# Gate stage of the second layer: key scaling, differences and shifts of the logs moved from VectorE to GpSimd

## What is computed

```python
def hgrn_gates(fx, lb):
    log_f = jnp.logaddexp(jnp.log(lb), jnp.log1p(-lb) + jax.nn.log_sigmoid(fx))
    k = (1.0 - lb) * jax.nn.sigmoid(-fx)
    return log_f, k
```

## Time and profile before

| | us |
|---|---|
| median of 3 runs | 4069.83 (4064.1 to 4074.27) |
| the profiled execution, its time | 4068.36 |
| its span | 4066.5 |
| PE busy | 3695.6 (91%) |
| VectorE (DVE) busy | 2607.3 (64%) |
| ScalarE (ACT) busy | 2022.8 (50%) |
| GpSimd (POOL) busy | 1042.4 (26%) |

### The profile page before, as it was taken

The page is one execution under the profiler, slowest core; times in us unless marked ns, Lnnn a source line. Parts: engine busy times, 40 slices in busy tenths (PEclk is TensorE's granted clock), DMA queues, the critical chain, the costliest instruction groups (busy, mean ns, idle before and its releaser), DMA issues. The chain is left out here.

```text
span 4066.5 us, 57429 instructions
## 1 busy us (share of the span) xinstructions
PE 3695.6 (91%) x21576; PEld 2898.5 (71%) x21576; DVE 2607.3 (64%) x3794; ACT 2022.8 (50%) x3880; POOL 1042.4 (26%) x1106
## 2 busy tenths in 40 slices
PE   6999898888999787888789999999898989999998
PEld 5775677777775676767466666678666768888886
DVE  3766567767765486776555555548966776665655
ACT  4544366655544286655344444456644554444444
POOL 0016103732017003610155555500281010111000
PEclk7989899999989898999899999999999999999999
DMA  5100113345200102351100000122003551111344
GB/s 192 42 16 1 39 52 112 129 154 189 69 21 1 54 21 99 119 182 54 31 5 7 9 6 6 36 81 80 9 5 138 189 154 42 60 44 42 110 155 150
DMA packets 211397, 295.44 MB, mean 73 GB/s; under 512 B 74218, under 2 KB 140010, under 8 KB 211124
## 3 DMA queue, kind: packets, MB, share of 16 engines
q1 hardware_dynamic: 210564, 291.57, 21.6%
q0 software_dynamic: 416, 0.05, 0.0%
q10 hardware_dynamic: 144, 0.15, 0.0%
HBM read 261.12 MB, written 30.51 MB: 72 GB/s over the span
## 5 line engine op out<-in xcount | busy, mean ns | idle before, releaser
L563 DVE TENSOR_TENSOR x_low<-buf_a,x_high 128x640 fp32r<-128x640 f32 (+5 forms) x360 | 359.9, 1000 | 307.3 <-ACT x_high L610 290.2
L610 ACT CAST x_high<-buf_a 128x640 fp32r<-128x640 f32 (+5 forms) x360 | 311.0, 864 | 394.8 <-PE ps L670 322.2
L668 PE MATMUL ps<-x_high,w_high 128*128 128x512 f32 (+1 forms) x1184 | 443.4, 375 | 61.5 <-DVE w_low L567 55.9
L669 PE MATMUL ps<-x_low,w_high 128*128 128x512 f32 (+1 forms) x1184 | 436.9, 369 | 0.0
L670 PE MATMUL ps<-x_high,w_low 128*128 128x512 f32 (+1 forms) x1184 | 436.0, 368 | 0.0
L3321 PE MATMUL ps<-w_high,x_high 128*128 128x512 f32 x896 | 362.4, 404 | 53.9 <-DVE w_low L3170 52.0
L3322 PE MATMUL ps<-w_low,x_high 128*128 128x512 f32 x896 | 356.1, 397 | 0.0
L3323 PE MATMUL ps<-w_high,x_low 128*128 128x512 f32 x896 | 355.7, 397 | 0.0
L3170 DVE TENSOR_TENSOR w_low<-w,w_high 128x1024 fp32r<-128x1024 f32 x170 | 226.4, 1332 | 172.7 <-ACT w_high L3262 172.7
L3905 DVE TENSOR_REDUCE mx<-ps 128x1 fp32r<-128x1280 f32 x128 | 190.7, 1491 | 200.2 <-PE ps L3780 199.7
L668 PEld LDWEIGHTS ps<-x_high,w_high 128*128 128x128 f32 x1184 | 226.6, 191 | 109.7 <-DVE x_low L563 64.6
(11 more groups left out here) (451 smaller groups left out, 8910.9 us busy)
## 6 DMA issues: line engine op xcount, KB each, us to landing
w<-in_w_out SPq DMA_DIRECT2D x26, 2048.0 KB, 8.4
w<-in_w_mod SPq DMA_DIRECT2D x24, 2048.0 KB, 9.1
w<-in_w_down SPq DMA_DIRECT2D x15, 2048.0 KB, 7.9
w<-in_w_in SPq DMA_DIRECT2D x26, 1024.0 KB, 5.2
w<-in_w_up SPq DMA_DIRECT2D x22, 1024.0 KB, 7.6
w<-in_w_in SPq DMA_DIRECT2D x6, 2048.0 KB, 8.8
x<-in_x SPq DMA_DIRECT2D x16, 512.0 KB, 8.9
scratch_h<-x SPq DMA_DIRECT2D x8, 512.0 KB
```

The costliest lines, as they stand in the source:

```text
L563: dve.tensor_tensor(part(xl, i)[:, 0:s["tn"]], x_of(s), part(xh, i)[:, 0:s["tn"]].bitcast(F32), ALU.subtract).then_inc(x_low, 1)
L610: act.copy(part(xh, i)[:, 0:s["tn"]], x_of(s)).then_inc(x_high, 1)
L668: pe.matmul(g["out"], lhs[0][:, :], rhs[0][:, :], start=(s["kk"] == 0), stop=False)
L669: pe.matmul(g["out"], lhs[0][:, :], rhs[1][:, :], start=False, stop=False)
```

## The change

The class `Gates` gets a program for GpSimd, issued in the same stage. In the second layer it takes over the key scalings (L3460), the additions (L3468) and the subtractions (L3469). The difference no longer reads the shifted logs: a new constant, row 3 minus row 4 of g, is put in row 7, and e = fx - row 7 is computed from the unshifted logs; the addition of row 4 to fx comes after it and is waited for only at L3475 (`moved_up`). VectorE waits for the difference (`differed`) before the absolute value. In the first layer GpSimd's program returns at once.

```diff
@@ class Beside
+    def pool(self, pool):
+        pass
@@ project_split
+        if beside:
+            @block.gpsimd
+            def _(pool):
+                beside.pool(pool)
@@ Gates.dve, bounds(i), i == KD
                 link(dve.tensor_tensor(g[:, 4, :], g[:, 7, :], g[:, 2, :], ALU.subtract))
+                link(dve.tensor_tensor(g[:, 7, :], g[:, 3, :], g[:, 4, :], ALU.subtract), self.bounded)
@@ Gates.dve, work(direction, o)
-            if self.LB and o in (2, 3):
-                c = o - 2
-                m = 2 * direction + c
-                dve.wait_ge(self.act_chain, acts + c + 1)
-                link(dve.tensor_scalar(key[:, :, c, :], key[:, :, c, :], g[:, 5, m:m + 1], None, ALU.mult))
             if o in (5, 6):
                 c = o - 5
                 dve.wait_ge(self.act_chain, acts + 5 + c)
-                link(dve.scalar_tensor_tensor(fx[:, c, :], fx[:, c, :], 0.0, e[c][:, :], ALU.min, ALU.subtract))
+                link(dve.scalar_tensor_tensor(fx[:, c, :], fx[:, c, :], 0.0, e[c][:, :], ALU.min, ALU.subtract), self.logs)
             if self.LB and o in (6, 7):
                 c = o - 6
                 m = 2 * direction + c
-                link(dve.tensor_scalar(fx[:, c, :], fx[:, c, :], g[:, 4, m:m + 1], None, ALU.add))
-                link(dve.tensor_scalar(e[c][:, :], fx[:, c, :], g[:, 3, m:m + 1], None, ALU.subtract))
+                dve.wait_ge(self.differed, m + 1)
                 link(dve.scalar_tensor_tensor(e[c][:, :], e[c][:, :], -1.0, e[c][:, :], ALU.mult, ALU.max), self.shifted)
             if self.LB and o in (self.added, self.added + 1):
                 dve.wait_ge(self.act_chain, acts + 9 + c)
+                dve.wait_ge(self.moved_up, m + 1)
                 link(dve.scalar_tensor_tensor(fx[:, c, :], fx[:, c, :], g[:, 3, m:m + 1], e[c][:, :], ALU.max, ALU.add))
@@ Gates
+    def pool(self, pool):
+        if not self.LB:
+            return
+        e, g = self.e, self.g
+        pool.wait_ge(self.bounded, 1)
+        for direction in range(2):
+            fx, key = self.a[direction], self.key[direction]
+            acts = self.n_init + self.n_dir * direction
+            for c in range(2):
+                m = 2 * direction + c
+                pool.wait_ge(self.act_chain, acts + c + 1)
+                pool.tensor_scalar(key[:, :, c, :], key[:, :, c, :], g[:, 5, m:m + 1], None, ALU.mult).then_inc(self.scaled, 1)
+            for c in range(2):
+                m = 2 * direction + c
+                pool.wait_ge(self.logs, m + 1)
+                pool.tensor_scalar(e[c][:, :], fx[:, c, :], g[:, 7, m:m + 1], None, ALU.subtract).then_inc(self.differed, 1)
+                pool.wait_ge(self.differed, m + 1)
+                pool.tensor_scalar(fx[:, c, :], fx[:, c, :], g[:, 4, m:m + 1], None, ALU.add).then_inc(self.moved_up, 1)
```

More of the change, by code:

```diff
@@ L3411, in __init__ @@
         self.g = lay("g", [P, 8, 4])
-        self.lb_in, self.dve_chain, self.bounds, self.magnitude, self.shifted, self.act_chain = self.sems = k.sems(
-            "bounds_in", "gates_dve_chain", "bounds_ready", "magnitude", "shifted", "gates_act_chain")
+        (self.lb_in, self.dve_chain, self.bounds, self.bounded, self.magnitude, self.logs, self.differed, self.shifted, self.moved_up, self.scaled,
+         self.act_chain) = self.sems = k.sems("bounds_in", "gates_dve_chain", "bounds_ready", "shifts_ready", "magnitude", "logs_done",
+                                              "differed", "shifted", "moved_up", "keys_scaled", "gates_act_chain")
         self.n_init, self.n_dir = (3, 10) if self.LB else (0, 6)
```

## The result

The changed kernel took 4091.53 us (median of 4 runs, 4087.6 to 4095.35) against 4066.97 (median of 4, 4059.33 to 4074.27) for the kernel before: ratio 1.0057, 95% interval 1.0041 to 1.0073, that is 17 to 30 us slower. The forecast was 4075.6 with a range up to 4090, and no change as the likeliest outcome. Both are wrong. The profiled execution took 4087.6 us (span 4085.8).

The account below looks back on a forecast made before the run. PE and, from 1494 to 1511, VectorE were taken to pace the stage; 10T - 9.2 with T = 1.5 us added 5.8 to the profiled 4068.36, giving 4074.2, and 1.5 to the median made 4075.6; range 4059 to 4090.

Parts of the forecast that it names:

- what bounds the stage: Second layer's projection stage: PE sets the pace where it has splits, VectorE from 1494 to 1511; at most some 12 us.
- the two engines take turns: Gate steps: while GpSimd runs, a VectorE instruction reading two SBUF tensors stands still, one whole instruction at a time.
- Rival 1: Second layer's gate stage: engines work side by side, so removed VectorE time counts; -8.0 us, 4061.8; chance 0.18.
- rival 2: Same stage: engines side by side and PE's clock stays up; -13.1 us, 4056.7, faster; chance 0.06.
- The sum 2 x (4T - 3.68) + 2T - 1.80: Shifts and differences of both directions plus key scalings of direction 1: 10T - 9.2, +5.8 us at T = 1.5.
- T: Time of one of the twelve GpSimd instructions of 128x1280 f32 in the stage; taken as 1.5 us.
- it is nearest to the cast, and I take T = 1.5 us: GpSimd's unseen one-tensor form priced between a cast (1.25 us) and two-tensor work (2.89), near the cast.
- The upper bound: GpSimd's new instruction takes at most the 2.89 us of an operation with two tensors and 1280 columns.
- rival 3: Shifts, both directions: GpSimd as slow as with two tensors, T = 2.89; +19.7 us, 4089.5, slower; chance 0.26.
- The sum by that rule, +1.5: By the skill's line rate at 1.2 GHz, T would be 1.07 us and the sum below +1.5 us.
- Cost: nothing: Key scalings of direction 0, about 1448 to 1453: 1.2 us more fits into 3.7 us of VectorE idle.
- the term 2 x (T - 0.90): Key scalings of direction 1, where VectorE has no idle: +1.2 us.

Follow-up runs that it names:

- copies: The changed kernel with each of GpSimd's twelve instructions replaced by a copy of the same tile: stage 159.4 us, +1.6 against before; kernel ratio 1.0013.
- beside_only: VectorE's program of the kernel before, plus twelve GpSimd tensor_scalar instructions on a tile nobody reads: stage 188.9 us, +31.1; one run, 4108.4 us.
- two_tensor: The changed kernel with GpSimd's twelve instructions as tensor_tensor with a broadcast column: stage 169.9 us, +12.1 against before; kernel ratio 1.0033.
- bench_prices: The kernel before plus an added first stage timing GpSimd forms alone and beside short VectorE instructions: tensor_scalar alone 3.53 us; unchanged gate stage 158.2 us.

## Why the prediction was wrong

**Right: what bounds the stage, and that the two engines take turns.** The forecast rested on the earlier trace rows, and the turns came as written: copies shows them instruction by instruction, and beside_only shows that they alone make the loss. Rival 1 (side by side) and with it rival 2 are out. The sum 2 x (4T - 3.68) + 2T - 1.80 holds, if T is read as the hold: with 1.08 us it gives +1.6 (measured +1.6, copies), with 2.1 us +11.8 (+12.1, two_tensor), with 2.80 us +18.8 (+18.2, the change). In the last, two small errors of the sum cancel: the second absolute value of direction 0 was held for 1.26 us and not 2.80, since the evictions had covered the rest, and the key scalings of direction 0 cost 1.2 us and not nothing.

**Wrong: "it is nearest to the cast, and I take T = 1.5 us".** This is the step that failed. T is 3.52 us alone, and its hold 2.80. I put an unseen form between two seen ones and picked by the number of tensors it reads. The form is what costs: tensor_scalar by a column takes 2.3 us more than a copy of the same tile, and 1.2 us more than the same product as a tensor_tensor with a broadcast column (2.32). Why tensor_scalar is so dear stays open. That VectorE stands still for the *whole* T was off too, the other way: with T = 3.52 the sum would have been +26.0. The upper bound failed as well: tensor_scalar is dearer than two-tensor work, 3.52 against 2.88 us. So rival 3 had the right mechanism and, since its 2.89 us is by accident close to the hold of 2.80, nearly the right time (+19.7 for +18.2). I gave it 0.26 and ended the range at its value, with nothing left for a longer T, so that the measured 4091.5 lies 1.5 us outside.

The Trainium skill's rule that GpSimd runs one-input work at roughly line rate ("GPSIMD Engine Reference", 4.1 Engine selection) is borne out for the copy (1.25 us for an estimated 1.07) and not for tensor_scalar (3.52). The sum by that rule, +1.5, lies near the +1.6 of copies by accident: the copy takes 1.25 us and holds VectorE for 1.08.

**Wrong in a small term: "Cost: nothing" for the key scalings of direction 0.** With 1.5 us they would have fitted into the idle; with holds of 1.85 and 2.79 they opened a gap of 2.03 us in PE at 1460 and cost about 1.2; 1.7 of their net surplus of 2.84 us did fit into the idle. In direction 1 the term 2 x (T - 0.90) is 5.55 - 1.80 = 3.75 us instead of 1.2.

**Wrong by a detail of the turns.** With the long instruction w_low at 1469.78 was not held, though GpSimd had been issued at 1468.67; the log behind it was. With copies w_low was held. The count of holds stays the same. In bench_prices, too, the short VectorE instruction that starts 0.04 us after GpSimd's tensor_scalar (28.38 against 28.34) keeps its 0.18 us, and the next one is held. Why one short instruction passes is not settled.

The kernel's own difference is 24.6 us between medians (17 to 30 by the interval) for 18.2 in the stage and 1.0 ahead of it in the profiles. The rest is within the scatter of the runs, which is some 15 us for the kernel before.

## What to carry to other kernels

An instruction moved from VectorE to GpSimd is not taken off VectorE where that engine has no idle and its work reads two tensors in SBUF or is a tensor_scalar, as here: compare GpSimd's *hold* with the VectorE duration that goes (here 2.80 us for 0.9), and the move pays only below that. Price the very form on GpSimd, alone, before moving it; copy, two tensors and tensor_scalar of one size lay at 1.25, 2.88 and 3.52 us. Look first at where the piece stands on VectorE itself: four additions put ahead of its idle made the stage 3.6 us shorter without another engine. To use idle GpSimd, look for stretches in which VectorE reads PSUM or reduces, or for work that only writes.

## What was unexpected of the hardware

- GpSimd's tensor_scalar of 128x1280 f32 takes 3.52 us by a column, 3.44 by a constant, 1.89 for half the columns; the same product as tensor_tensor with a broadcast column takes 2.32, less than with two real tensors (2.88).
- VectorE is held for 2.80 of 3.52 us (tensor_scalar), 2.69 of 2.88 (two tensors), 1.09 of 1.25 (copy) and not at all beside a memset. Its own one-tensor tensor_scalar is held longer than its tensor_tensor: 3.26 us in bench_prices, 3.14 to 3.16 in beside_only.
- A held instruction appears in the profile as busy, not as waiting: VectorE showed 20 us more busy time with 11 instructions fewer. The surplus over the same instruction elsewhere is the only sign.
